# Thirty additions of a 31-tap convolution move from VectorE to GpSimd

## Chip, cores and metric

The kernel runs on one core of one Trainium2 chip. The metric is device time in microseconds of one execution; lower is better. All arithmetic is float32 or float32r, and all inputs start in HBM.

## What is computed

Two transformer blocks over the same 256 tokens of width 2048: the first with latent attention, sliding-window attention and an MLP, the second with a mixer, cross-attention and an MLP. The change lies in the mixer, whose one half is a depthwise convolution of width 31 over 1024 channels:

```python
def causal_depthwise_conv(x, w):
    """x (B, T, C), w (W, C): y[t, c] = sum_j w[j, c] * x[t - (W-1) + j, c] (zero left padding)."""
...
    c = glu[..., :D_CONV] * jax.nn.sigmoid(glu[..., D_CONV:])
    c = causal_depthwise_conv(c, cf_dw_w) + cf_dw_b
    c = jax.nn.silu(layer_norm(c, cf_ln_g, cf_ln_b))
    return jnp.concatenate([o, c], axis=-1) @ w_out
```

`o` is the other half: a gated delta rule over 8 heads, behind a convolution of width 4 on q, k and v.

## The kernel before, in words

**The stream of weights.** The time is spent on some 430 slots of weights, 1 MB each, loaded through SyncE's queue into `Wt`. A slot is worked off in two halves. For each half ScalarE makes a rounded copy `WH` (L1881), VectorE the remainder `WL` = `Wt` - `WH` (L2630), and TensorE multiplies three ways (L1267, L1268, L1269; L1305 and L1306 where the product is turned). `WH` and `WL` have four buffers (`NR = 4`), so the split of a half waits until TensorE has finished the half four before it.

**The order of the rest.** A planner (`Plan`) writes one list of steps; each engine's program walks the list and issues, in that order, what is its own of each step. Between two halves `pump` advances every background generator by one `yield`. All other work (norms, attention, convolutions, the delta rule) is such background, and it reaches an engine at a fixed place between the splits. An engine executes strictly in its program's order.

**The convolution.** `conv31` has steps k = 0 to 59. Step k is tap j = 1 + k // 2 on channel tiles 0 to 3 (g = 0, even k) or 4 to 7 (g = 1, odd k). The accumulator `AC` holds 8 tiles of 256 tokens. In `conv_tap` ScalarE writes w\*x of four tiles into a product buffer `PRD` (L2201), of which there are two; in `conv_add` VectorE adds it into `AC` (L3148), one planner step later. Above `SHARED` = 18 the odd steps don't use ScalarE: VectorE multiplies and adds each of the four tiles itself (L3153). So VectorE has 39 additions at L3148 (30 even steps, and the odd steps 1 to 17) and 84 at L3153. A generator variable `slow` sets how many halves lie between two steps: four at first, two near the end of `w_in_2`, one from the start of the delta rule. `cln_fold` sums `AC` when the last two steps are in.

**Neighbours in the same stretch.** While `w_in_2` streams, `qkv` runs six groups. In each, VectorE does three taps (L3167), ScalarE an exponential and a logarithm, VectorE a minimum (L3175, tile `QE`), ScalarE an exponential (L2251), VectorE a product (L3182), and for the q and k groups ScalarE a square (L2268) and TensorE a sum over channels (L1569); the two v groups go from L3182 straight to TensorE (L1559). While the next product streams, `gen_delta` inverts triangular blocks: TensorE (L1655), ScalarE (L2398) and VectorE (L3429, L3432) in turn, one short product after another between the halves. SyncE only issues loads and GpSimd's program is empty.

Of the kernel before, what the change touches and what calls it, by code (L numbers as in the profile page):

```python
# [16 lines left out]
ADD, SUB, MUL, MAX, MIN = ALU.add, ALU.subtract, ALU.mult, ALU.max, ALU.min  # L17
# [11 lines left out]
SHARED = 18  # L29
# [63 lines left out]
class Marks:  # L93
# [7 lines left out]
    def up(self, sig, *key, by=1, frees=None):  # L101
        n = self.count[sig] = self.count.get(sig, 0) + by
        self.value[(sig, *key)] = n
        for use in () if frees is None else frees if isinstance(frees, (list, tuple)) else (frees,):
            self.emptied.setdefault(use.n, {})[sig] = n
        return (self.sems and self.sems[sig]), by
# [12 lines left out]
    def at(self, sig, *key):  # L119
        if self.counted is None:  # L120
            return sig, None, 0
        return sig, self.sems[sig], self.counted.value[(sig, *key)]

    def last(self, sig):
        return sig, (self.sems and self.sems[sig]), self.count.get(sig, 0)
# [1086 lines left out]
    return [({"lnm1": "evwo.v", "lnxa": "evwo2.v", "lnm2": "evxo.v"}[nm], c, tb)]  # L1212

def q_tile(h):

    return sorted({(192 * h) // 512, (0, 0, 1, 1, 1, 2, 2, 2)[h]})
# [7 lines left out]
def tensor_program(pe, on, m, M, plan):  # L1225
# [243 lines left out]
    @named  # L1469
    def mla_turn(h, hq, b0, b1):  # L1470
        st, bk = f"mla{h % 6}", m.bank(b0)
        for s in freed(b0):
            on.wait_ge(*s)
        for c in q_tile(h):
            on.wait_ge(*at("evq.a", c))
            on.wait_ge(*at("evq.v", c))
        for tb in range(2):
            pe.transpose(bk[:, tb * P:(tb + 1) * P], m.Q[:, tb, 192 * h:192 * h + 128], ident)
        on.wait_ge(*at("rope.v", hq))
        for tb in range(2):  # L1480
            t = pe.transpose(bk[:, 256 + tb * P:256 + (tb + 1) * P], m.Q[:, tb, 192 * h + 64:192 * h + 192], ident)
        t.then_inc(*up(st + ".t", "queries", h))
        bk = m.bank(b1)
        on.wait_ge(*at("evkv.a", h // 2))
        on.wait_ge(*at("evkv.v", h // 2))
        for s in freed(b1):
            on.wait_ge(*s)
        for tb in range(2):
            t = pe.transpose(bk[:, tb * P:(tb + 1) * P], m.KV[:, tb, 256 * h:256 * h + 128], ident)
        t.then_inc(*up(st + ".t", "keys", h))  # L1490
# [344 lines left out]
def scalar_program(act, on, m, M, plan):  # L1835
    up, at, last, freed, dma = M.up, M.at, M.last, M.freed, M.dma
# [350 lines left out]
    @named  # L2187
    def conv_tap(k, j, g):
        if k > SHARED and g:
            return  # L2190
        if k == SHARED:
            on.wait_ge(*at("cconv.v", "added", k - 1))
        elif k > SHARED + 2:
            on.wait_ge(*at("cconv.v", "added", k - 4))
        elif k >= 2:
            on.wait_ge(*at("cconv.v", "added", k - 2))
        on.wait_ge(*at("mix.a", "turned", 1, 1))
        on.wait_ge(*at("prep.v", "columns"))
        for i in range(4):
            w = 8 * j + 4 * g + i  # L2200
            act.activation(m.products(k)[:, i, :], m.CP[:, 4 * g + i, j:j + 256], ACT.Copy, scale=m.CFW[:, w:w + 1]  # L2201
                           ).then_inc(*up("cconv.a", k))
# [380 lines left out]
def vector_program(dve, on, m, M, plan):  # L2583
    up, at, last = M.up, M.at, M.last
# [556 lines left out]
    @named  # L3141
    def conv_add(k, j, g):

        cs = slice(4 * g, 4 * g + 4)
        on.wait_ge(*(at("cconv.v", "added", k - 2) if k >= 2 else at("cconv.v", "first", g)))
        if k <= SHARED or g == 0:
            on.wait_ge(*at("cconv.a", k))
            dve.tensor_tensor(m.AC[:, cs, :], m.AC[:, cs, :], m.products(k)[:, :, :], ADD).then_inc(  # L3148
                *up("cconv.v", "added", k))
            return  # L3150
        for i in range(4, 8):
            w = 8 * j + i
            dve.scalar_tensor_tensor(m.AC[:, i, :], m.CP[:, i, j:j + 256], m.CFW[:, w:w + 1], m.AC[:, i, :], MUL, ADD  # L3153
                                     ).then_inc(*up("cconv.v", "added", k))
# [84 lines left out]
    @named  # L3239
    def cln_fold():  # L3240
        for k in (58, 59):
            on.wait_ge(*at("cconv.v", "added", k))
        dve.tensor_tensor(m.LNA[:, 0:4, :], m.AC[:, 0:4, :], m.AC[:, 4:8, :], ADD).then_inc(*up("cln.v"))
        on.wait_ge(*last("cln.v"))
        dve.tensor_tensor(m.LNA[:, 0:2, :], m.LNA[:, 0:2, :], m.LNA[:, 2:4, :], ADD).then_inc(*up("cln.v"))
        on.wait_ge(*last("cln.v"))
        dve.tensor_tensor(m.LNA[:, 0, :], m.LNA[:, 0, :], m.LNA[:, 1, :], ADD).then_inc(*up("cln.v", "folded"))
# [352 lines left out]
            step[name](*args)  # L3600

def sync_program(sp, on, m, M, plan):
    at, dma = M.at, M.dma
    A, step = m.A, {}
# [117 lines left out]
def build(nc, A, out):  # L3723
    m = Memory(nc, A, out)
    plan = plan_all(A)
    programs = (sync_program, scalar_program, vector_program, tensor_program)
    counted = Marks()
    for program in programs:
        program(Counting(), Waits(Counting()), m, counted, plan)
    with ExitStack() as ctx:  # L3730
        sems = {n: ctx.enter_context(nc.semaphore(n.replace(".", "_"))) for n in counted.count}
        M = Marks(counted, sems)
        block = ctx.enter_context(nc.Block())
        block.sync(lambda e: sync_program(e, Waits(e), m, M, plan))
        block.scalar(lambda e: scalar_program(e, Waits(e), m, M, plan))
        block.vector(lambda e: vector_program(e, Waits(e), m, M, plan))
        block.tensor(lambda e: tensor_program(e, Waits(e), m, M, plan))

NAMES = ["x", "positions", "rel_bias", "attn_norm", "w_in", "q_a_norm", "w_q_b", "kv_a_norm", "w_kv_b", "sinks",  # L3740
# [27 lines left out]
```

## Time and profile before

| what | value |
|---|---|
| median of 3 runs | 2580.25 us (2579.12 to 2581.32) |
| profiled execution | 2579.72 us |
| its span, first to last instruction | 2577.9 us |
| TensorE busy | 2550.9 us (99%) |
| VectorE busy | 1659.1 us (64%), 2130 instructions |
| ScalarE busy | 1332.1 us (52%) |
| GpSimd busy | 0.2 us, 4 instructions |
| granted TensorE clock | 0.998 |

Busy time counts an engine's instructions. Idle time before an instruction is put down to the instruction that released its semaphore; TensorE's records overlap a little, since its instructions are pipelined. The profile shows no time for the start of an execution and its end, 1.8 us here, beside the span. On VectorE, records overlap too: an addition of 128x1024 has 1.216 us on record, and the next instruction starts 1.14 us after it.

### The profile page before, as it was taken

Reading aid. Unit: us, or ns where it says so; the run is one execution under the profiler, and the core shown is the slowest. Engines: PE = TensorE matmul, PEld = TensorE weight load, DVE = VectorE, ACT = ScalarE, POOL = GpSimd, SP = SyncE. Lnnn points to the kernel's source line nnn. Section 1 sums busy time; section 2 is a strip of 40 time slices with the busy share of each in tenths; the row PEclk is TensorE's granted clock in tenths of the full one; section 3 lists DMA queues with packets and bytes.
Section 4 is the critical chain, followed back from the end, with each engine's and each line's share of the span. In section 5 each row is a group of like instructions: output and inputs, shape, how many; then the busy total and the mean of one; then the engine's idle time right before and its main releaser. Section 6 shows DMA issues by size and latency. Waiting matters only on the chain.

```text
span 2577.9 us, 33743 instructions
## 1 busy us (share of the span) xinstructions
PE 2550.9 (99%) x13752; PEld 2153.1 (84%) x13752; DVE 1659.1 (64%) x2130; ACT 1332.1 (52%) x1885; POOL 0.2 (0%) x4
## 2 busy tenths in 40 slices
PE   9999999999999999999999999999999999999998
PEld 8878888888888888887788888888888888888887
DVE  8686566655665567568887986544556555665565
ACT  6565554444444446568866665544554444444444
POOL 0000000000000000000000000000000000000000
PEclk9999999999999999999999999999999999999999
DMA  6534666565566555555453446544655556556554
GB/s 228 171 122 146 214 225 200 193 196 188 190 194 194 188 190 180 196 180 168 138 195 131 148 147 253 188 140 146 200 192 189 188 196 194 186 191 196 193 186 144
DMA packets 235041, 470.77 MB, mean 183 GB/s; under 512 B 8235, under 2 KB 17158, under 8 KB 233478
## 3 DMA queue, kind: packets, MB, share of 16 engines
q1 hardware_dynamic: 234134, 467.04, 55.0%
q8 instruction: 108, 1.77, 0.3%
q10 hardware_dynamic: 752, 1.58, 0.2%
q14 instruction: 47, 0.39, 0.0%
HBM read 462.30 MB, written 6.29 MB: 182 GB/s over the span
## 4 chain that ended last, share of the span: by engine, by line
PE 48%; DVE 1%; ACT 1%; issue 1%; DVEq 0%; ACTq 0%
PE ps L1267 10%; PE ps L1269 10%; PE ps L1268 10%; PE ps L1306 9%; PE ps L1305 5%; PE ps L1655 1%; PE ps L1826 1%; PE ps L1801 1%; PE ps L1338 0%; DVE WL L2630 0%; DVE AC L3153 0%; PE ps L1737 0%; ACT WH L1881 0%; PE ps L1638 0%; PE ps L1700 0%
## 5 line engine op out<-in xcount | busy, mean ns | idle before, releaser
L2630 DVE TENSOR_TENSOR WL<-Wt,WH 128x1024 fp32r<-128x1024 f32 (+1 forms) x861 | 1037.0, 1209 | 707.4 <-ACT WH L1881 651.7
L1881 ACT ACTIVATE WH<-Wt 128x1024 fp32r<-128x1024 f32 (+1 forms) x861 | 894.1, 1046 | 780.1 <-PE ps L1269 517.1
L1267 PE MATMUL ps<-WH,XT 128*128 128x512 f32 (+1 forms) x1184 | 470.6, 398 | 0.3 <-DVE XT L3028 0.3
L1267 PE MATMUL ps<-WH,HT 128*128 128x512 f32 (+2 forms) x1176 | 456.6, 388 | 3.3 <-DVE WL L2630 3.3
L1269 PE MATMUL ps<-WH,XT 128*128 128x512 f32 (+1 forms) x1184 | 459.8, 388 | 0.0
L1268 PE MATMUL ps<-WL,XT 128*128 128x512 f32 (+1 forms) x1184 | 459.3, 388 | 0.0
L1269 PE MATMUL ps<-WH,HT 128*128 128x512 f32 (+2 forms) x1176 | 451.4, 384 | 0.0
L1268 PE MATMUL ps<-WL,HT 128*128 128x512 f32 (+2 forms) x1176 | 451.0, 384 | 0.0
L1306 PE MATMUL ps<-XT,WH 128*128 128x512 f32 x960 | 336.5, 394 | 0.0
L1306 PE MATMUL ps<-HT,WH 128*128 128x512 f32 x960 | 336.5, 394 | 0.0
L1305 PE MATMUL ps<-XT,WL 128*128 128x256 f32 x960 | 266.6, 278 | 0.0
L1305 PE MATMUL ps<-HT,WL 128*128 128x256 f32 x960 | 266.6, 278 | 0.0
L1269 PEld LDWEIGHTS ps<-WH,XT 128*128 128x128 f32 x1184 | 222.6, 188 | 46.4
L1267 PEld LDWEIGHTS ps<-WH,XT 128*128 128x128 f32 x1184 | 222.8, 188 | 44.7 <-DVE XT L3028 0.7
L1267 PEld LDWEIGHTS ps<-WH,HT 128*128 128x128 f32 x1176 | 220.8, 188 | 46.4 <-DVE WL L2630 4.8
L1268 PEld LDWEIGHTS ps<-WL,XT 128*128 128x128 f32 x1184 | 223.0, 188 | 42.6
L1269 PEld LDWEIGHTS ps<-WH,HT 128*128 128x128 f32 x1176 | 220.7, 188 | 42.7
L1268 PEld LDWEIGHTS ps<-WL,HT 128*128 128x128 f32 x1176 | 220.9, 188 | 42.4 <-issue 1.0
L1306 PEld LDWEIGHTS ps<-XT,WH 128*128 128x128 f32 x960 | 180.0, 188 | 39.0
L1306 PEld LDWEIGHTS ps<-HT,WH 128*128 128x128 f32 x960 | 180.0, 188 | 39.0
L1305 PEld LDWEIGHTS ps<-HT,WL 128*128 128x128 f32 x960 | 180.3, 188 | 2.9
L1305 PEld LDWEIGHTS ps<-XT,WL 128*128 128x128 f32 x960 | 180.3, 188 | 2.9
(412 smaller groups left out, 1863.0 us busy)
## 6 DMA issues: line engine op xcount, KB each, us to landing
Wt<-in_mlp_w SPq DMA_DIRECT2D x128, 1024.0 KB, 5.1
Wt<-in_w_up SPq DMA_DIRECT2D x64, 1024.0 KB, 5.3
Wt<-in_w_down SPq DMA_DIRECT2D x64, 1024.0 KB, 5.0
Wt<-in_w_in SPq DMA_DIRECT2D x53, 1024.0 KB, 5.0
Wt<-in_w_out SPq DMA_DIRECT2D x32, 1024.0 KB, 5.0
Wt<-in_xa_wk SPq DMA_DIRECT2D x16, 1024.0 KB, 5.1
Wt<-in_xa_wv SPq DMA_DIRECT2D x16, 1024.0 KB, 5.0
Wt<-in_xa_wq SPq DMA_DIRECT2D x16, 1024.0 KB, 5.1
```

Source lines behind the costliest of these rows:

```text
L1267: pe.matmul(o, xh, wh, start=start, stop=False)
L1268: pe.matmul(o, xh, wl, start=False, stop=False)
L1269: done = pe.matmul(o, xl, wh, start=False, stop=stop)
L1305: pe.matmul(*(both if start else one), start=start, stop=False)
L1306: done = pe.matmul(*(one if start else both), start=False, stop=stop)
L1655: done = pe.matmul(m.bank(use)[r, 64 * h:64 * h + 64], left(r, h), right(r, h), start=True, stop=True)
L1801: t = pe.matmul(m.bank(b)[:, tb * 256:(tb + 1) * 256], m.QXT[:, u, k, tb * P:(tb + 1) * P], m.XKT[:, 4 * h + k, :], start=k == 0, stop=k == 3)
L1826: t = pe.matmul(m.bank(b)[:, i * 256:(i + 1) * 256], m.XV[:, mb, c:c + P], m.PXT[:, h % 2, mb, :], start=mb == 0, stop=mb == 1)
L1881: act.activation(m.WH[:, i % NR, 0:2 * w], m.Wt[:, slot % NW, h * 2 * w:(h + 1) * 2 * w], ACT.Copy).then_inc(*up("wsplit.a", i))
L2630: dve.tensor_tensor(m.WL[:, i % NR, 0:2 * w], m.Wt[:, slot % NW, h * 2 * w:(h + 1) * 2 * w], m.WH[:, i % NR, 0:2 * w].bitcast(F32), SUB).t ...
```

## The change

GpSimd gets a program of its own, `pool_program`. It walks the same list and does `conv_add` for the even steps (channel tiles 0 to 3), 30 additions of 128x1024, each counted on a new semaphore `cconv.p`. VectorE's `conv_add` returns at once for g = 0. ScalarE's `conv_tap` waits for the addition that last read its product buffer, on GpSimd's or VectorE's semaphore (`conv_added`), and `cln_fold` waits for step 58 on GpSimd's and 59 on VectorE's.

```diff
+def conv_added(k):
+    return "cconv.v" if k % 2 else "cconv.p", "added", k
...
         if k == SHARED:
-            on.wait_ge(*at("cconv.v", "added", k - 1))
-        elif k > SHARED + 2:
-            on.wait_ge(*at("cconv.v", "added", k - 4))
+            on.wait_ge(*at(*conv_added(k - 1)))
+        if k > SHARED + 2:
+            on.wait_ge(*at(*conv_added(k - 4)))
         elif k >= 2:
-            on.wait_ge(*at("cconv.v", "added", k - 2))
+            on.wait_ge(*at(*conv_added(k - 2)))
...
     def conv_add(k, j, g):
-        cs = slice(4 * g, 4 * g + 4)
+        if g == 0:
+            return
         on.wait_ge(*(at("cconv.v", "added", k - 2) if k >= 2 else at("cconv.v", "first", g)))
-        if k <= SHARED or g == 0:
+        if k <= SHARED:
             on.wait_ge(*at("cconv.a", k))
-            dve.tensor_tensor(m.AC[:, cs, :], m.AC[:, cs, :], m.products(k)[:, :, :], ADD).then_inc(
+            dve.tensor_tensor(m.AC[:, 4:8, :], m.AC[:, 4:8, :], m.products(k)[:, :, :], ADD).then_inc(
                 *up("cconv.v", "added", k))
...
     def cln_fold():
         for k in (58, 59):
-            on.wait_ge(*at("cconv.v", "added", k))
+            on.wait_ge(*at(*conv_added(k)))
...
+def pool_program(pool, on, m, M, plan):
+    up, at = M.up, M.at
+    def conv_add(k, j, g):
+        if g:
+            return
+        on.wait_ge(*(at("cconv.p", "added", k - 2) if k >= 2 else at("cconv.v", "first", 0)))
+        on.wait_ge(*at("cconv.a", k))
+        pool.tensor_tensor(m.AC[:, 0:4, :], m.AC[:, 0:4, :], m.products(k)[:, :, :], ADD).then_inc(
+            *up("cconv.p", "added", k))
+    for name, args in plan.steps:
+        if name == "conv_add":
+            conv_add(*args)
...
+        block.gpsimd(lambda e: pool_program(e, Waits(e), m, M, plan))
```

How the instructions stand. Lines of the changed kernel are 5 or 6 higher than the same ones before. First VectorE's program beside the second and third `qkv` group, where steps 3 and 4 of the convolution stood; `PRD0` holds even steps and `PRD1` odd ones here. Before:

```order
L2630 TENSOR_TENSOR WL_51<-Wt_49,WH_50 128x1024 [waits wsplit_a]
L3148 TENSOR_TENSOR AC_140<-AC_140,PRD1_149 128x1024 [waits cconv_a,cconv_v]
L3175 SCALAR_TENSOR_TENSOR QE1_146<-QA1_144,QE1_146 128x1024 [waits qkv_a]
...
L3182 TENSOR_TENSOR QA1_144<-QA1_144,QE1_146 128x1024 [waits qkv_a]
...
L2630 TENSOR_TENSOR WL_51<-Wt_49,WH_50 128x1024 [waits gemm_t,wsplit_a]
L3148 TENSOR_TENSOR AC_140<-AC_140,PRD0_148 128x1024 [waits cconv_a,cconv_v]
L3167 SCALAR_TENSOR_TENSOR QA0_143<-QC_142,DNW_58,QA0_143 128x256 [waits qkv_v] x4
```

and changed:

```order
L2635 TENSOR_TENSOR WL_51<-Wt_49,WH_50 128x1024 [waits wsplit_a]
L3154 TENSOR_TENSOR AC_140<-AC_140,PRD1_149 128x1024 [waits cconv_a,cconv_v]
L3181 SCALAR_TENSOR_TENSOR QE1_146<-QA1_144,QE1_146 128x1024 [waits qkv_a]
...
L3188 TENSOR_TENSOR QA1_144<-QA1_144,QE1_146 128x1024 [waits qkv_a]
...
L2635 TENSOR_TENSOR WL_51<-Wt_49,WH_50 128x1024 [waits gemm_t,wsplit_a]
L3173 SCALAR_TENSOR_TENSOR QA0_143<-QC_142,DNW_58,QA0_143 128x256 [waits qkv_v] x4
```

The even addition (from `PRD0`) is gone; the odd one still stands ahead of the minimum. Second, VectorE's program in the delta rule's second block, late in the convolution. Before:

```order
L2630 TENSOR_TENSOR WL_51<-Wt_49,WH_50 128x1024 [waits gemm_t,wsplit_a,wload1]
L3327 TENSOR_SCALAR KVS_165<-ps3,SM_65 128x512 [waits st_kx,gemm_t]
L3429 TENSOR_TENSOR XS5_159<-XS4_158,CST_55 128x512
L3432 TENSOR_TENSOR E0_162<-CST_55,ps6 128x512 [waits delta_t]
L3148 TENSOR_TENSOR AC_140<-AC_140,PRD1_149 128x1024 [waits cconv_a,cconv_v]
L2630 TENSOR_TENSOR WL_51<-Wt_49,WH_50 128x1024 [waits wsplit_a]
```

and changed:

```order
L2635 TENSOR_TENSOR WL_51<-Wt_49,WH_50 128x1024 [waits gemm_t,wsplit_a,wload1]
L3333 TENSOR_SCALAR KVS_165<-ps3,SM_65 128x512 [waits st_kx,gemm_t]
L3435 TENSOR_TENSOR XS5_159<-XS4_158,CST_55 128x512
L3438 TENSOR_TENSOR E0_162<-CST_55,ps6 128x512 [waits delta_t]
L2635 TENSOR_TENSOR WL_51<-Wt_49,WH_50 128x1024 [waits wsplit_a]
```

The addition behind `E0` is gone; what TensorE waits for (`E0`) stood ahead of it already. Third, GpSimd's new program from its start:

```order
L3618 ISA
L3618 TENSOR_TENSOR AC_140<-AC_140,PRD0_148 128x1024 [waits cconv_a,cconv_v]
L3618 TENSOR_TENSOR AC_140<-AC_140,PRD0_148 128x1024 [waits cconv_a,cconv_p] x8
L3618 TENSOR_TENSOR AC_140<-AC_140,PRD1_149 128x1024 [waits cconv_a,cconv_p]
L3618 TENSOR_TENSOR AC_140<-AC_140,PRD0_148 128x1024 [waits cconv_a,cconv_p]
```

An addition there is bound to no place among VectorE's instructions: it may start as soon as ScalarE's four products are written.

## Rows read from the trace of the kernel before

**Rows 1.** The page, busy time by engine: us, share of the span, instructions.
```profile
PE 2550.9 (99%) x13752; PEld 2153.1 (84%) x13752; DVE 1659.1 (64%) x2130; ACT 1332.1 (52%) x1885; POOL 0.2 (0%) x4
```

**Rows 2.** Tile PRD: duration ns min/median/max, first and last start us, forms.
```profile
L2201 ACT ACTIVATE PRD<-CP,CFW x156: 489/496/512, 1135.0 to 1484.6; 128x256 f32<-128x256 f32 x156
L3148 DVE TENSOR_TENSOR AC<-AC,PRD x39: 1212/1216/1225, 1147.9 to 1489.0; 128x1024 f32<-128x1024 f32 x39
```

**Rows 3.** Windows from 1147 us: busy us by engine, clock, DMA share, GB/s.
```profile
1147.00:1257.00 110.00, 110.00 (x495) 89.10 (x494) 90.14 (x118) 92.30 (x135) 0.00 (x0) 1.00 0.50 160
1340.00:1495.00 155.00, 153.06 (x1546) 126.78 (x1545) 135.56 (x195) 96.36 (x162) 0.00 (x0) 1.00 0.44 145
1147.00:1495.00 348.00, 340.52 (x2497) 287.13 (x2496) 292.35 (x407) 247.89 (x402) 0.00 (x0) 1.00 0.48 156
```

**Rows 4.** TensorE's waits, 1134 to 1552 us: total us, times, longest.
```profile
PE ps L1267 <- DVE WL L2630: 3.3, 4, 1.5
PE ps L1559 <- DVE QA L3182: 2.3, 2, 1.4
PE ps L1655 <- DVE XS L3421: 1.5, 1, 1.5
PE ps L1587 <- DVE LNA L3247: 1.3, 1, 1.3
PE ps L1761 <- DVE VT L3504: 1.0, 1, 1.0
PE ps L1737 <- DVE XS L3469: 0.5, 1, 0.5
```

**Rows 5.** Timeline, one qkv group, VectorE and ScalarE: start us, us, instruction [idle before].
```profile
1185.49 1.22 DVE L3148 TENSOR_TENSOR AC<-AC,PRD 128x1024 f32<-128x1024 f32 x1
1186.62 1.22 DVE L3175 SCALAR_TENSOR_TENSOR QE<-QA,QE 128x1024 f32<-128x1024 f32 x1
...
1184.22 1.70 ACT L2201 ACTIVATE PRD<-CP,CFW 128x256 f32<-128x256 f32 x4
...
1187.87 1.06 ACT L2251 ACTIVATE QE<-QE 128x1024 f32<-128x1024 f32 x1 [1.01 <-DVE QE L3175]
...
1193.29 1.06 ACT L2268 ACTIVATE QE<-QA 128x1024 f32<-128x1024 f32 x1
```

**Rows 6.** The same group on TensorE.
```profile
1194.87 1.88 PE L1569 MATMUL ps<-QE,CST 128*128 128x512 f32 x4
```

**Rows 7.** Timeline, delta rule, ScalarE and VectorE, 1465 to 1480 us.
```profile
1465.37 1.70 ACT L2201 ACTIVATE PRD<-CP,CFW 128x256 f32<-128x256 f32 x4
...
1474.38 1.70 ACT L2201 ACTIVATE PRD<-CP,CFW 128x256 f32<-128x256 f32 x4
...
1468.62 1.22 DVE L2630 TENSOR_TENSOR WL<-Wt,WH 128x1024 fp32r<-128x1024 f32 x1 [0.89 <-issue]
...
1471.02 0.68 DVE L3432 TENSOR_TENSOR E<-CST,ps 128x512 f32<-128x512 f32 x1
1471.62 1.22 DVE L3148 TENSOR_TENSOR AC<-AC,PRD 128x1024 f32<-128x1024 f32 x1
...
1477.11 1.23 DVE L2630 TENSOR_TENSOR WL<-Wt,WH 128x1024 fp32r<-128x1024 f32 x1 [0.95 <-issue]
...
1478.85 0.68 DVE L3432 TENSOR_TENSOR E<-CST,ps 128x512 f32<-128x512 f32 x1
```

**Rows 8.** The same stretch on TensorE: where it takes what L3432 made.
```profile
1471.75 1.15 PE L1655 MATMUL ps<-E,XS 64*64 64x64 f32 x32
...
1480.74 1.15 PE L1655 MATMUL ps<-E,XS 64*64 64x64 f32 x32
```

**Rows 9.** Timeline, VectorE, where narrow halves follow each other.
```profile
1268.68 1.22 DVE L3148 TENSOR_TENSOR AC<-AC,PRD 128x1024 f32<-128x1024 f32 x1
1269.82 1.66 DVE L3167 SCALAR_TENSOR_TENSOR QA<-QC,DNW,QA 128x256 f32<-128x256 f32 x4
1271.40 0.88 DVE L2630 TENSOR_TENSOR WL<-Wt,WH 128x704 fp32r<-128x704 f32 x1
```

More of the change, by code:

```diff
@@ L3725, in build @@
     plan = plan_all(A)
-    programs = (sync_program, scalar_program, vector_program, tensor_program)
+    programs = (sync_program, scalar_program, vector_program, tensor_program, pool_program)
     counted = Marks()
```

## Prediction

> **What bounds the kernel now.** I read the page first. TensorE is busy for 2550.9 of 2577.9 us and VectorE for 1659.1 [rows 1]: a microsecond taken off VectorE is worth something only where TensorE waits for it. So I read TensorE's waits in the stretch of the convolution: 3.3 + 2.3 + 1.5 + 1.3 + 1.0 + 0.5 = 9.9 us, all for VectorE [rows 4]. That is the most that a faster VectorE can give back. Then the windows: from the first addition to the last, VectorE is busy for 292.35 of 348 us, TensorE for 340.52 [rows 3]. VectorE is not the bound, but it has no more than 56 us to spare in 348, and TensorE's program takes many of its results in the middle of the stream. The question is then how much a handover can slip before TensorE feels it, and for that I read timelines.
>
> In a `qkv` group the reader should see a chain without slack. VectorE's minimum starts at 1186.62 and ends at 1187.84; ScalarE's exponential, which had stood idle for it for 1.01 us, starts at 1187.87; the product and the square follow, and the square ends at 1193.29 + 1.06 = 1194.35, 0.52 us ahead of TensorE's sum at 1194.87 [rows 5, 6]. A slip of the minimum by more than about half a microsecond therefore stands in TensorE's way. In the delta rule VectorE's L3432 ends at 1471.70 and TensorE takes it at 1471.75, a slack of 0.05 us; the next time it ends at 1479.53 and is taken at 1480.74, a slack of 1.21 us [rows 7, 8]. This pair repeats every 9 us or so.
>
> **The change, part by part.**
>
> *Taken from VectorE:* 30 of the 39 additions at L3148, 1.216 us each on record [rows 2], 1.14 us each from start to start (1268.68 to 1269.82 [rows 9]): 30 x 1.14 = 34 us less work. By itself this shortens the kernel only at the waits. One removed addition stands ahead of the narrow split at 1271.40 [rows 9], at the head of the 3.3 us of waits for `WL`: -1.1. The waits for L3421 (1.5) and for L3247, the fold of the convolution (1.3), each have removed additions right ahead on VectorE: -1.5 and -1.1. L3469: -0.5. Sum -4.2; the bounds are 0 and -9.9 [rows 4]. I take -5, since an earlier VectorE also starts ScalarE's answers earlier.
>
> *Put on GpSimd:* 30 additions of 128x1024 with both inputs in SBUF. The trace holds no work of this engine but four tiny fills [rows 1], so its price has to be bounded. Not under VectorE's 1.2 us for the same work [rows 2]. ScalarE passes the same elements with a single input in 1.70 us for four tiles [rows 5]. The additions read twice that, and I take twice VectorE's time, 2.4 us, as an estimate. Upwards, 3.6 us (three times VectorE's) is my bound. The engine itself is in no hurry: its additions come 24 us apart beside the `qkv` groups and 9.0 us apart in the delta rule (ScalarE's products at 1465.37 and 1474.38 [rows 7]), so at 2.4 us no product buffer is late, and what waits for it costs 0. Its start-up instruction runs at the beginning, over 1100 us ahead of the first addition: 0.
>
 The asymmetry speaks for it: what is freed is worth 5 us at best guess, and even a hold of half the addition, 1.2 us, eats all of the 1.14 us that the addition freed, and comes at a moment that ScalarE chooses and not VectorE's program.
>
> Where would the hold fall? Beside the `qkv` groups: ScalarE's product for an even step ends at 1184.22 + 1.70 = 1185.92 [rows 5]. GpSimd's addition then stands right ahead of the minimum at 1186.62, in every group, since both come every eight halves. The minimum is 2.4 us late, less the slack of 0.5: 1.9 us at TensorE. Six groups: 6 x 1.9 = 11.4 us. In the delta rule: 18 of the additions fall there, one for each 9 us. The first of the two shown would start at 1467.07, right ahead of the split due at 1468.62 [rows 7]; it ends at 1469.5, the split and L3432 behind it are 0.9 us late, and with a slack of 0.05 all of it reaches TensorE. Where VectorE is still busy when the products are done, the hold starts later and costs up to 1.4. The second would run from 1476.08 to 1478.5 against a split due at 1477.11: 1.4 us late, slack 1.21, so 0.2 at TensorE. The mean of 1.4 and 0.2 is 0.8: 18 x 0.8 = 14.4 us. The other six additions lie where halves follow each other with several microseconds in hand: 0. Sum of the holds 25.8 us; with the relief, 25.8 - 5 = +21 us.
>
> **The sum** against the profiled execution: 2579.7 + 21 = 2600.7 us. That execution is 0.5 us under the median of 2580.25, so 2601 us.
>
> The Trainium skill, SBUF — State Buffer, section Who interferes with whom, says that a VectorE instruction with two SBUF inputs contends with a GpSimd instruction that reads SBUF, whichever starts second being blocked for the whole of the first. No run here shows it so far; it is the upper end above. Its page GPSIMD Engine Reference, section 3.1, gives 4497 ns for such an addition of twice the length; half of that, 2.25 us as an estimate from that page, would make the holds 0.15 us shorter and the sum about 3 us less.
>
> **Rivals.**
>
> *1. No hold: VectorE is simply relieved.* For it: ScalarE's products beside busy VectorE stay within 489 to 512 ns [rows 2], so engines can work side by side on SBUF. Against it: nothing in the trace; that pair of engines just isn't shown. Mechanism: the 1.14 us gone ahead of the split at 1271.40, ahead of L3421 and ahead of the fold. Time: 2580.25 - 5 = 2575 us, at the very most 2570. It decides if a GpSimd addition delays VectorE by less than about 0.3 us. This is the case of the other sign.
>
> *2. The two share, and each is slowed.* A GpSimd addition beside VectorE costs it about 1.2 us, as much as it gave up. VectorE's sum is unchanged, but the delay comes ahead of the minimum and of L3432 where the freed addition had stood behind them. `qkv`: 1.2 - 0.5 = 0.7, six times 4 us; delta rule: 0.2 x 18 = 4; less 5: +3, 2583 us. This is no measurable difference: 0.2% of the time, 5.2 us, is about what a measurement of this kernel can tell from no change.
>
> *3. The hold is full and a GpSimd addition is longer.* At 3.6 us: 6 x 3.1 = 19, and in the delta rule 18 x 2.0 = 36, since slack covers none of what is added; less 5: +50, 2630 us. Beyond 8.9 us ScalarE would wait for product buffers too. Nothing in the trace speaks for it.
>
> **How the numbers follow.** Full hold at about 2.4 us, my forecast (2590 to 2613): 0.52. Rival 3: 0.12. Rival 2: 0.14, of which a third above 5.2 us. Rival 1: 0.22, of which two thirds gain over 5.2 us, since its -5 sits on that line and -9.9 is its end. Faster: 0.15. Slower: 0.52 + 0.12 + 0.04 = 0.68. Within 0.2%: 0.17. The range runs from 2573, which leaves out the last few in 100 of rival 1, to 2624, which leaves out most of rival 3.
>
> **What would show it.** In the profile after: 30 GpSimd additions of 2 to 2.6 us; VectorE's L3175 or the split next to it standing 1 to 2 us longer or later than its 1.22 us; new waits of TensorE at L1569 (none before) of about 2 us four times, and at L1655 of up to 1.4 us many times; VectorE's other rows unchanged. Wrong it is if VectorE's instructions beside a GpSimd addition start and end as before: then 2575. If TensorE's waits grow but the delay per addition is not near GpSimd's duration, the size was wrong, not the mechanism.

## The result and the profile after

| | before | changed |
|---|---|---|
| median of 4 runs each | 2580.3 us | 2602.73 us |
| span of the profiled execution | 2577.9 us | 2601.2 us |
| ratio, 95% interval | | 1.0091 [1.0079, 1.0103] |

The change makes the kernel slower by 0.9%, 22.4 us by the medians; 2601 us had been forecast. The page after, busy time by engine, against [rows 1]:

```profile
PE 2554.3 (98%) x13752; PEld 2153.5 (83%) x13752; DVE 1673.2 (64%) x2100; ACT 1331.8 (51%) x1885; POOL 80.9 (3%) x34
```

VectorE has 30 instructions less and 14 us more on record. The tile `PRD` shows both engines' additions (duration ns min/median/max), against [rows 2]:

```profile
L3618 POOL TENSOR_TENSOR AC<-AC,PRD x30: 2367/2404/4480, 1137.6 to 1507.8; 128x1024 f32<-128x1024 f32 x30
L3154 DVE TENSOR_TENSOR AC<-AC,PRD x9: 1217/1218/1219, 1161.9 to 1324.0; 128x1024 f32<-128x1024 f32 x9
```

A GpSimd addition takes twice VectorE's time. The second of the six qkv groups, VectorE's timeline with GpSimd's addition beside it, against [rows 5] (start us, us):

```profile
1188.15 1.22 DVE L3154 TENSOR_TENSOR AC<-AC,PRD 128x1024 f32<-128x1024 f32 x1
1189.29 3.43 DVE L3181 SCALAR_TENSOR_TENSOR QE<-QA,QE 128x1024 f32<-128x1024 f32 x1
1192.65 1.21 DVE L2635 TENSOR_TENSOR WL<-Wt,WH 128x1024 fp32r<-128x1024 f32 x1
```

```profile
1188.72 2.92 POOL L3618 TENSOR_TENSOR AC<-AC,PRD 128x1024 f32<-128x1024 f32 x1 [23.35 <-ACT PRD L2206]
```

GpSimd's instruction is dispatched at 1188.72, while VectorE adds; it has 2.92 us on record where one that meets nobody has 2.38, so it was kept waiting for about 0.5 us, until VectorE's addition was over at 1189.37. Then it is VectorE's turn: the minimum has 3.43 us on record in place of 1.22. It ends at 1192.72, 1.08 us after GpSimd's end at 1191.64: it did its own work only then. ScalarE and TensorE behind it, against [rows 5, 6]:

```profile
1192.76 1.06 ACT L2256 ACTIVATE QE<-QE 128x1024 f32<-128x1024 f32 x1 [3.23 <-DVE QE L3181]
```

```profile
1199.27 1.99 PE L1574 MATMUL ps<-QE,CST 128*128 128x512 f32 x4 [1.57 <-ACT QE L2273]
```

That is the whole mechanism in one piece: hold, late minimum, late exponential, late square, TensorE idle. The minimum is struck in all six groups (ns):

```profile
L3181 DVE SCALAR_TENSOR_TENSOR QE<-QA,QE x6: 3386/3422/3434, 1163.0 to 1290.3; 128x1024 f32<-128x1024 f32 x6
```

Before, it read

```profile
L3175 DVE SCALAR_TENSOR_TENSOR QE<-QA,QE x6: 1215/1217/1218, 1162.2 to 1281.0; 128x1024 f32<-128x1024 f32 x6
```

TensorE's waits over the whole execution, total, times, longest, against [rows 4] (the largest, and the last ones of the stretch):

```profile
PE ps L1272 <- DVE WL L2635: 8.1, 5, 3.7
PE ps L1660 <- DVE E L3438: 7.0, 6, 2.0
PE ps L1574 <- ACT QE L2273: 6.3, 4, 1.6
PE ps L1660 <- DVE XS L3420: 2.4, 2, 2.1
PE ps L1564 <- DVE QA L3188: 1.9, 1, 1.9
...
PE ps L1766 <- DVE VT L3510: 1.0, 1, 1.0
PE ps L1592 <- DVE LNA L3253: 1.0, 1, 1.0
PE ps L1660 <- DVE XS L3427: 0.7, 2, 0.4
...
PE ps L1742 <- DVE XS L3475: 0.5, 1, 0.5
```

The nine sum to 28.9 us where [rows 4] had 9.9: 19.0 of the span's 23.3. Of the rest, 0.8 us lies before the convolution, in the start of this execution. Most of the remainder stands at the waits themselves: at the first sum TensorE idles for 1.59 us on record and falls 2.0 us behind. One stretch at the lower clock level adds a little, of which more below.

Where the time came from is best seen by when TensorE begins the same half of weights in both traces. The table holds that shift in us against the kernel before, worked out from one execution of each: the start of TensorE's first weight load of the half after, less the same before; ahead of the convolution (first column) it shows what an execution's start differs by. Times in the heading are those of the kernel before.

| kernel | 1124 us | 1172 | 1262 | 1288 | 1342 | 1445 | 1506 | end |
|---|---|---|---|---|---|---|---|---|
| changed | 0.8 | 2.7 | 10.0 | 11.9 | 11.9 | 20.2 | 23.0 | 23.2 |
| e2_none | -1.0 | -1.0 | -1.0 | -2.2 | -2.2 | -2.1 | -4.0 | -3.8 |
| e1_writes | -1.1 | -1.1 | -1.1 | -0.8 | -0.8 | -0.8 | -2.7 | -2.5 |
| e6_early | 0.7 | 2.6 | 9.9 | 12.0 | 12.0 | 12.0 | 12.0 | 12.0 |
| e7_late | -0.4 | -0.4 | -0.4 | -0.4 | -0.4 | 9.3 | 12.1 | 12.1 |
| e4_after_product | -1.1 | -1.1 | 1.2 | 4.6 | 6.1 | 14.4 | 17.3 | 17.3 |
| e8_gate | -1.5 | -1.4 | 1.0 | 2.5 | 2.5 | 7.0 | 8.1 | 8.1 |
| e5_quarters | 0.3 | 0.5 | 1.7 | 3.0 | 3.0 | 6.4 | 9.9 | 9.9 |
| e9_one_input | 0.5 | 1.1 | 2.8 | 4.0 | 4.0 | 4.0 | 2.1 | 2.3 |
| e10_gate_quarters | 1.1 | 1.1 | 2.9 | 4.2 | 4.2 | 5.8 | 8.0 | 8.0 |
| e11_twice | 0.3 | 2.3 | 12.3 | 14.4 | 21.0 | 52.0 | 68.4 | 68.6 |

The changed kernel loses 9.2 us in five steps of 1.6 to 2.0 us, one for each qkv group up to 1262 us, 1.9 more with the sixth, nothing up to 1342, and 11.1 us in the delta rule. There the loss is uneven: TensorE's waits range from 0.3 to 2.2 us, and several of the 18 additions cause none.

### The profile page after: what moved, and what is told of

It reads as the page before. It is cut to its first block and busy times, and to the rows that moved or that the text cites. A ratio compares the mean times of both kernels' runs of the same rounds, so it can differ in the third digit from the quotient of the medians.

```text
span 2601.2 us, 33746 instructions
## 1 busy us (share of the span) xinstructions
PE 2554.3 (98%) x13752; PEld 2153.5 (83%) x13752; DVE 1673.2 (64%) x2100; ACT 1331.8 (51%) x1885; POOL 80.9 (3%) x34
## 5 line engine op out<-in xcount | busy, mean ns | idle before, releaser
L2635 DVE TENSOR_TENSOR WL<-Wt,WH 128x1024 fp32r<-128x1024 f32 (+1 forms) x861 | 1056.2, 1232 | 715.0 <-ACT WH L1886 655.1
```

The lines of the kernel that those rows point to most:

```text
L2635: dve.tensor_tensor(m.WL[:, i % NR, 0:2 * w], m.Wt[:, slot % NW, h * 2 * w:(h + 1) * 2 * w], m.WH[:, i % NR, 0:2 * w].bitcast(F32), SUB).t ...
```

## The experiments

All are edits of the changed kernel; the name in brackets is the one in the table. Each was timed beside the kernel before, and its ratio is to that: medians of 2579.07 us for `e2_none`, `e1_writes`, `e6_early` and `e4_after_product`, 2578.73 us for `e9_one_input`, `e7_late`, `e8_gate` and `e5_quarters`, 2579.85 us for the last two. Against the changed kernel's 2602.73 us, taken beside 2580.3 us, they are best compared by what each is above its own.

**Take the additions away, leave the signals** (`e2_none`). The edit:

```diff
-        pool.tensor_tensor(m.AC[:, 0:4, :], m.AC[:, 0:4, :], m.products(k)[:, :, :], ADD).then_inc(
-            *up("cconv.p", "added", k))
+        pool.nop().then_inc(*up("cconv.p", "added", k))
```

> GpSimd's program keeps its waits and its signals, but the 30 additions of channel tiles 0 to 3 are left out on every engine, so the convolution of those tiles lacks taps 1 to 30. What is left is the relief of VectorE alone. Hold theory (a GpSimd addition keeps VectorE's instructions with two SBUF inputs waiting): about 2575 us, 5 under before, and all of the 27 us up to the changed kernel's 2602.7 is what the additions on GpSimd cost. Rival (the new semaphores and the other order of waits cost the time, not the additions): it stays near 2600.

Measured: 2577.14 us, ratio to before 0.999 [0.9981, 0.9999]. The new semaphores and orders cost nothing; all of the loss is what the additions do on GpSimd. The relief by itself is small, 2.8 us by the table and 1.9 us by the medians. TensorE's waits in the stretch, total, times, longest:

```profile
PE ps L1272 <- DVE WL L2635: 2.6, 2, 1.5
PE ps L1564 <- DVE QA L3188: 2.3, 2, 1.4
PE ps L1766 <- DVE VT L3510: 1.0, 1, 1.0
PE ps L1592 <- DVE LNA L3253: 1.0, 1, 1.0
PE ps L1742 <- DVE XS L3475: 0.5, 1, 0.5
```

Against [rows 4], only the wait for L3421 (1.5) went as a whole; the splits gave 0.7 on record (1.1 by the shift) and the fold 0.3.

**Keep GpSimd busy, but let it only write** (`e1_writes`).

```diff
-        pool.tensor_tensor(m.AC[:, 0:4, :], m.AC[:, 0:4, :], m.products(k)[:, :, :], ADD).then_inc(
+        for _ in range(2):
+            pool.memset(m.AC[:, 0:4, :], 0.0).then_inc(*up("cconv.p"))
+            on.wait_ge(*M.last("cconv.p"))
+        pool.memset(m.AC[:, 0:4, :], 0.0).then_inc(
             *up("cconv.p", "added", k))
```

> Each GpSimd addition is replaced by three fills of the same 128x1024 in a row, each waited for: GpSimd is as busy in the same places, writes SBUF but reads nothing from it. The sums of tiles 0 to 3 are left out. If what holds VectorE is the reading of SBUF by GpSimd: no VectorE row is stretched and the time is that of the kernel without additions, about 2575 us. If any GpSimd access to SBUF holds it (rival): VectorE's minimum takes 1.2 us plus the rest of a fill, and with fills of 1 us each the time is 2585 to 2600.

Measured: 2578.22 us, ratio 0.9996 [0.9987, 1.0005], 1.1 us above the kernel without additions. GpSimd was as busy as with additions (86 us of fills), and the minimum was not touched, though it ran beside the fills:

```profile
1184.94 1.97 POOL L3620 MEMSET AC<- 128x1024 f32 x2 [21.44 <-ACT PRD L2207]
1186.97 0.96 POOL L3622 MEMSET AC<- 128x1024 f32 x1
```

```profile
1185.54 1.22 DVE L3182 SCALAR_TENSOR_TENSOR QE<-QA,QE 128x1024 f32<-128x1024 f32 x1
```

So it is GpSimd's reading of SBUF that holds the minimum, not its work and not its writing. No other instruction of VectorE with 128x256 elements or more was longer beside a fill either. But writing alone is not free: three small instructions for the delta rule's gates are stretched beside the fills of the sixth group. A `TENSOR_SCALAR` of 128x16 with a single input in SBUF lasts until the fill ends, twice:

```profile
1279.92 0.59 DVE L3205 TENSOR_SCALAR SM<-SM 128x16 f32<-128x16 f32 x1
...
1280.57 0.95 DVE L3210 TENSOR_SCALAR SM<-SM 128x16 f32<-128x16 f32 x1
```

```profile
1278.52 1.97 POOL L3620 MEMSET AC<- 128x1024 f32 x2 [17.57 <-ACT PRD L2207]
1280.55 0.95 POOL L3622 MEMSET AC<- 128x1024 f32 x1
```

Without additions the first of them reads

```profile
1279.97 0.17 DVE L3204 TENSOR_SCALAR SM<-SM 128x16 f32<-128x16 f32 x1
```

The split behind them is 1.1 us late, and TensorE waits 2.6 us for it where it waited 1.5. That is most of the 1.4 us by which the table parts the two kernels at 1288 us, and as much as parts their medians, which the intervals don't separate. A stretch at the lower clock level follows in this execution, of which below.

**Read one input in place of two** (`e9_one_input`).

```diff
-        pool.tensor_tensor(m.AC[:, 0:4, :], m.AC[:, 0:4, :], m.products(k)[:, :, :], ADD).then_inc(
+        pool.tensor_scalar(m.AC[:, 0:4, :], m.products(k)[:, :, :], 1.0, None, MUL).then_inc(
             *up("cconv.p", "added", k))
```

> Each GpSimd addition is replaced by a multiplication by 1.0 of the product buffer into the same tiles of AC: one SBUF input in place of two, the sum of tiles 0 to 3 is left out. If GpSimd's reading holds VectorE for as long as the instruction runs, the cost follows its duration: at 1.3 us a hold of about 1.1, qkv groups 6 x 0.7, delta rule about 3, relief 5: 2580 to 2586 us. If only an instruction with two inputs holds VectorE (rival): 2575 us and no VectorE row is stretched.

Measured: 2580.48 us, ratio 1.0005 [0.9996, 1.0015]. That lies in the 2580 to 2586 us expected, and can't be told from the kernel before. The reason given does not hold, though. The instruction is longer than the addition, and holds less:

```profile
L3618 POOL TENSOR_SCALAR AC<-PRD x30: 2770/2777/4841, 1137.4 to 1487.7; 128x1024 f32<-128x1024 f32 x30
```

```profile
L3181 DVE SCALAR_TENSOR_TENSOR QE<-QA,QE x6: 2058/2060/2062, 1162.7 to 1283.1; 128x1024 f32<-128x1024 f32 x6
```

```profile
1187.10 3.28 POOL L3618 TENSOR_SCALAR AC<-PRD 128x1024 f32<-128x1024 f32 x1 [21.63 <-ACT PRD L2206]
```

The minimum is held for 0.84 us, and its work is done at 1189.72, 0.66 us before GpSimd's instruction ends at 1190.38. For this instruction the hold ends well before its end; with two inputs it lasted until the end. Why is not shown.

**Only early, only late** (`e6_early`, `e7_late`). A function decides by k which engine adds an even step; VectorE has the others as before.

```diff
+def on_pool(k):
+    return k % 2 == 0 and k <= 12        # e7_late: k >= 14
...
-        on.wait_ge(*(at("cconv.v", "added", k - 2) if k >= 2 else at("cconv.v", "first", g)))
+        on.wait_ge(*(at(*conv_added(k - 2)) if k >= 2 else at("cconv.v", "first", g)))
```

> GpSimd takes the even steps up to 12 only; VectorE has those from 14 on as before. The convolution's additions beside the qkv groups are then the only ones on GpSimd. Sum of the prediction: 6 holds of 1.9 us less about 1 us of relief, +10 us, 2590 us (the trace of the changed kernel has +9 to +11 there). Rival (cost spread evenly over the 30 additions): 7/30 of 22.4, +5 us, 2585.

> GpSimd takes the even steps from 14 on only, 23 additions; those beside the qkv groups are on VectorE as before. Place theory: the delta rule's share of the changed kernel, +11 to +12 us, 2592 us, and with the early half (GpSimd for steps up to 12) it adds up to the +22 of both. Rival (even spread): 23/30 of 22.4, +17 us, 2597.

Measured: 2591.08 us (ratio 1.0045 [1.0030, 1.0060]) and 2591.14 us (1.0044 [1.0028, 1.0061]). Seven additions beside the qkv groups cost as much as 23 later ones: place counts, not number. The shifts of 11.3 and 12.5 us from the convolution's start add up to 23.8, the changed kernel's is 22.4. TensorE's largest waits, early first:

```profile
PE ps L1578 <- ACT QE L2277: 6.3, 4, 1.6
```

```profile
PE ps L1664 <- DVE E L3443: 7.1, 6, 2.0
```

**Move the hold behind the product** (`e4_after_product`).

```diff
         on.wait_ge(*at("cconv.a", k))
+        if 2 <= k <= 12:
+            on.wait_ge(*at("qkv.v", "mul", k // 2 - 1))
```

> Beside the six qkv groups (steps 2 to 12) GpSimd's addition also waits for VectorE's product of that group, so it can no longer stand ahead of the minimum. The hold falls on the split and the taps of the next group, where there are some 3 us in hand. Place theory: the five steps of 1.8 us at TensorE's sums vanish, about 9 us less than the changed kernel, 2593 to 2595 us, no wait at the sum over channels. Rival (what counts is VectorE's total of work and hold, wherever the hold falls): within 3 us of 2602.7.

Measured: 2597.21 us, ratio 1.0073 [1.0056, 1.0090]: 5.5 us less than the changed kernel, and 18.1 above its own before in place of 22.4, so 4 rather than 9 us less. The minimum is back at its old length, and the waits at the sums go from 6.3 to 1.4 us:

```profile
L3181 DVE SCALAR_TENSOR_TENSOR QE<-QA,QE x6: 1217/1220/1220, 1161.1 to 1283.6; 128x1024 f32<-128x1024 f32 x6
```

```profile
PE ps L1584 <- DVE SM L3224: 1.7, 1, 1.7
PE ps L1574 <- ACT QE L2273: 1.4, 3, 0.6
```

By the table the shift up to 1262 us is 2.3 in place of 9.2. But from there to 1342 it is 4.9 in place of 1.9: where narrow halves follow each other VectorE has nothing in hand, and a hold hurts anywhere. A new wait of 1.7 us, for a small result of the gates, is part of it, and the last 1.5 us are a stretch at the lower clock level right behind that wait.

**Start no earlier than VectorE did** (`e8_gate`). VectorE notes its newest signal where it added before, and GpSimd waits for it.

```diff
         if g == 0:
+            M.gate[k] = M.newest
             return
...
         on.wait_ge(*at("cconv.a", k))
+        if M.counted:
+            sig, n = M.counted.gate[k]
+            on.wait_ge(sig, M.sems[sig], n)
```

> Each GpSimd addition also waits for the VectorE instruction ahead of which... behind which VectorE did that addition before. It can no longer start early in the middle of a chain; VectorE loses up to 2.4 us where it had spent 1.14. Place theory: the qkv share vanishes (the taps follow, with slack) and of the delta rule's share the part stays in which VectorE is behind anyway: +3 to +8 us, 2583 to 2588. Rival (total of hold counts): 2600.

Measured: 2587.98 us, ratio 1.0035 [1.0022, 1.0048], at the end of what was expected. Same additions, same hold (four taps take 3.82 us in place of 1.67), but 9.3 us above its own before in place of 22.4:

```profile
1197.00 3.82 DVE L3176 SCALAR_TENSOR_TENSOR QA<-QC,DNW,QA 128x256 f32<-128x256 f32 x4
```

**Cut each addition in four** (`e5_quarters`).

```diff
-        pool.tensor_tensor(m.AC[:, 0:4, :], m.AC[:, 0:4, :], m.products(k)[:, :, :], ADD).then_inc(
-            *up("cconv.p", "added", k))
+        for i in range(4):
+            t = pool.tensor_tensor(m.AC[:, i, :], m.AC[:, i, :], m.products(k)[:, i, :], ADD)
+        t.then_inc(*up("cconv.p", "added", k))
```

> Each GpSimd addition is cut into four of 128x256. If a hold lasts for one GpSimd instruction and VectorE gets in between two of them, a VectorE instruction is held by 0.7 us at most at a time: a minimum of 1.2 us takes at most 2 us on record, the slack of 0.5 covers most, and the time is 2585 to 2592. If GpSimd keeps VectorE out over its whole queue of four (rival), the row of the minimum shows 3.4 us or more and the time is 2602 to 2606, a bit above the changed kernel for the four starts.

Measured: 2588.55 us, ratio 1.0036 [1.0023, 1.0049], 9.8 us above its own before. The engines take turns: four quarters need 5.31 us, and each of VectorE's two instructions beside them is held by 0.54 us:

```profile
1186.56 5.31 POOL L3619 TENSOR_TENSOR AC<-AC,PRD 128x256 f32<-128x256 f32 x4 [19.32 <-ACT PRD L2206]
```

```profile
1187.12 1.76 DVE L3181 SCALAR_TENSOR_TENSOR QE<-QA,QE 128x1024 f32<-128x1024 f32 x1
1188.81 1.76 DVE L2635 TENSOR_TENSOR WL<-Wt,WH 128x1024 fp32r<-128x1024 f32 x1
```

A hold of 0.54 is about the slack of 0.5 us that the chain had, and up to 1262 us the shift is 1.4 us in place of 9.2.

**Both mendings** (`e10_gate_quarters`, the two edits above together).

> Both mendings at once: each addition in four of 128x256, and none before VectorE has reached the place where it did that addition before. If a late start and a short hold save different parts, less than either alone (2588.0 and 2588.6 us): 2581 to 2585. If they save the same part (rival), 2587 or 2588. Under the kernel before by more than 0.2% by neither: the kernel without any additions on GpSimd was only 2 us under it.

Measured: 2585.76 us, ratio 1.0024 [1.0014, 1.0033]: 5.9 us above its own before, 2 to 4 us better than either edit alone, 1 us above the expected stretch, and still slower than before. No version with these additions on GpSimd came under the kernel before.

**Each addition twice** (`e11_twice`).

```diff
+        pool.tensor_tensor(m.AC[:, 0:4, :], m.AC[:, 0:4, :], m.products(k)[:, :, :], ADD).then_inc(*up("cconv.p"))
+        on.wait_ge(*M.last("cconv.p"))
         pool.tensor_tensor(m.AC[:, 0:4, :], m.AC[:, 0:4, :], m.products(k)[:, :, :], ADD).then_inc(
```

> Each GpSimd addition is done twice, the second once the first has signalled, so tiles 0 to 3 get each product twice. Hold theory: VectorE gets in between the two (as it does between quarters), so the minimum shows 3.4 us as before and the instruction behind it is held as well, 2.4 us. In the qkv groups that hits a split with 3 us in hand, in the delta rule mostly a split that L3432 stands behind. The cost grows by more than a quarter and less than double: 2610 to 2630 us. Rival (what costs is that the first addition cuts in at a bad moment, later ones are free): under 2607.

Measured: 2650.06 us, ratio 1.0273 [1.0257, 1.0288]: three times the cost, where less than double was expected. Beside the qkv groups the second addition cost little: the shift up to 1262 us is 12.0 in place of 9.2. The miss is in the delta rule, 47.4 us in place of 11.1, with 6.6 more between 1288 and 1342 us, where single additions had cost nothing. TensorE's largest waits:

```profile
PE ps L1272 <- DVE WL L2635: 21.2, 9, 5.7
PE ps L1660 <- DVE E L3438: 21.2, 10, 2.8
```

VectorE now falls behind with the splits as well, and the windows (busy us of PE, PEld, DVE, ACT, POOL, then the granted clock) show a second cost:

```profile
1147.00:1540.00 393.00, 341.85 (x2294) 285.19 (x2294) 340.41 (x361) 239.46 (x388) 158.32 (x55) 0.95 0.41 136
```

The clock is granted at 0.95 where [rows 3] have 1.00. Over 393 us that is worth up to 20 us. In the delta rule the record has seven stretches at 1.2 GHz, 27.3 us long in all, and while they last the shift grows by some 11.6 us. So about a quarter of the 47.4 us is clock and the rest is waits.

## Why the prediction was right

*The bound.* TensorE's waits for VectorE, 9.9 us, were to be the most that relief can give. It gave 2.8 us (shift of e2_none), forecast at 5. Of the four terms, the split's 1.1 came (by the shift) and L3421 gave its 1.5; the fold gave 0.3 in place of 1.1, L3469 nothing, and the 0.8 added on top for ScalarE's earlier answers wasn't there. Ahead of the fold the waiting moved on to another input: in `e2_none` VectorE stands idle for 0.73 us until TensorE has the results that its copy L3447 takes. Ahead of L3469 no addition stood at all; VectorE had been idle for 4.6 us before the split and the one instruction that stand ahead of it.

*GpSimd's price.* 2.4 us was taken, 2.38 to 2.40 measured. Its first addition had 4.48 us, and a split dispatched 1.0 us after that one's start was not held (1.22 us); why is open. The additions come as close as 3.5 us in the delta rule, not every 9.0 us, and ScalarE still never waits for one. Rival 3 (3.6 us) is out.

*The hold.* Full, as taken: 3.42 us for the minimum. It begins when VectorE's own addition is over, so 2.2 of the 2.4 us fall on the minimum. The choice of the upper end is now a measured one; when it was made it rested on asymmetry alone. Rival 1 (no hold) and rival 2 (shared, 1.2 us each) are out by that row, and only without additions did the time come near rival 1's 2575 us.

The Trainium skill, SBUF — State Buffer, section Who interferes with whom, states the contention for VectorE instructions with two SBUF inputs against GpSimd instructions that read SBUF, not against those that only write: the trace agrees on both halves (3.42 us beside additions, 1.22 beside fills). The section calls the shared ports an exclusive lock, and writes of blocking for the whole instruction where it treats VectorE's 2-port modes. That whoever starts second is blocked for the whole of the first agrees for the addition, but not for the one-input instruction, whose 2.78 us held VectorE for 0.84.

*Beside the qkv groups.* 6 x 1.9 = 11.4 us was the term. Measured 9.2 for five groups and 1.9 net with the sixth, 11.1 in all. The slack of 0.5 us read from one group's timeline held for the four q and k groups, where TensorE waits 1.57 to 1.59 us at the sum. The fifth and sixth have no sum: there the split behind the minimum came late (waits of 1.45 us, and of 3.66 where it had been 1.50), and that the cost is about the same is luck. Luck is in the 2.4 us too: an addition from 1185.92 on would end at 1188.32, 1.7 us after the minimum was due, not 2.4. The rest came because VectorE's odd addition kept GpSimd's waiting first, which the prediction does not say.

*In the delta rule.* 18 x 0.8 = 14.4 us less most of the relief was the term, 11.1 measured net. At the first of the two sample places the hold fell on the four instructions of VectorE's odd step at L3159, 3.78 us in place of 1.66, not on the split behind them, and TensorE waited 1.08 us for `E` (1.4 forecast). At the second the split was held (2.57 us), and `E` still came in time (0.2 forecast):

```profile
1487.33 3.78 DVE L3159 SCALAR_TENSOR_TENSOR AC<-CP,CFW,AC 128x256 f32<-128x256 f32 x4
...
1499.52 2.57 DVE L2635 TENSOR_TENSOR WL<-Wt,WH 128x1024 fp32r<-128x1024 f32 x1 [2.09 <-issue]
...
1502.62 0.67 DVE L3438 TENSOR_TENSOR E<-CST,ps 128x512 f32<-128x512 f32 x1
```

```profile
1494.16 1.15 PE L1660 MATMUL ps<-E,XS 64*64 64x64 f32 x32 [1.08 <-DVE E L3438]
...
1503.35 1.15 PE L1660 MATMUL ps<-E,XS 64*64 64x64 f32 x32
```

The mean of two places came out right for the whole, though single waits reach 2.15 us and several additions cost nothing.

*The other six* were to cost nothing, and did: one addition lies ahead of the first qkv group, five between 1288 and 1342 us, where the shift stays at 11.9 although they hold VectorE too.

The sum: holds 25.8 forecast, 25.2 measured (22.4 + 2.8 of shift); relief 5 forecast, 2.8 measured. A hold 0.6 us too large makes up for part of a relief 2.2 us too large, and the forecast is 1.6 us short.

## What to carry to other kernels

Work moved from VectorE to GpSimd is not free work on an idle engine: while a GpSimd addition reads SBUF, VectorE's next instruction with two SBUF inputs stands still, so 1.14 us freed was paid with 2.2 us at a moment that the program's order doesn't choose. Before such a move, find where GpSimd's instruction will start (its releaser, not its place in the plan) and what VectorE instruction stands there, and read the slack from it to TensorE. If it must be done, short GpSimd instructions started behind the tight handover cost a quarter of long early ones (5.9 against 22.4 us). Fills left VectorE's large instructions alone; what they held were small ones of the gates, 1.1 us at TensorE.

## What the runs showed of the hardware beyond what was expected

*Only some VectorE instructions are held.* Beside GpSimd additions, those with one input in PSUM kept their length: the four at L3394 (`XS` from `ps` and `XS`), two of them started within an addition, and `E` from `CST` and `ps` at 1405.5 us:

```profile
L3394 DVE TENSOR_TENSOR XS<-ps,XS x4: 674/679/684, 1337.6 to 1448.4; 128x512 f32<-128x512 f32 x4
```

A single input doesn't protect where it is in SBUF: the small `TENSOR_SCALAR` of the gates was held by fills (0.95 us in place of 0.17), and by the additions of `e11_twice` for 2.14 us.

*The hold of a one-input GpSimd instruction is shorter than the instruction* (0.84 us at the minimum, of 2.78).

*TensorE's idle time can come back as a lower clock.* After its longest wait, 3.66 us, the changed kernel shows a stretch at 1.2 in place of 2.4 GHz, 3.4 us long by the clock's record and 0.79 of full speed in the window of 8 us around it; matmuls of 352 columns go from 0.32 to 0.50 us. The kernel before has none there.

```profile
1295.12 0.43 PE L1272 MATMUL ps<-WH,HT 128*128 128x352 f32 x1 [3.66 <-DVE WL L2635]
1295.39 0.38 PE L1273 MATMUL ps<-WL,HT 128*128 128x352 f32 x1
1295.56 0.50 PE L1274 MATMUL ps<-WH,HT 128*128 128x352 f32 x1
```

```profile
1292.00:1300.00 8.00, 4.88 (x25) 4.82 (x25) 6.82 (x14) 5.96 (x14) 0.57 (x1) 0.79 0.34 104
```

At half speed for 3.4 us it could cost 1.7 us. Here the shift grows by 1.1 us in it, and a wait for `QA` of 0.90 us, which the kernel before has right behind, takes nearly all of that up. In `e7_late`, where no such wait follows, a stretch cost 1.5 us. One execution each is no proof that the wait brings it about. The fills' execution had such a stretch too, at 1282 us in a wait of 2.6 us, and the one without additions, whose longest wait was 1.5 us, had none in the convolution. But the length of the wait does not decide alone: stretches follow waits of 1.68 us (`e4_after_product`) and 1.93 us (`e7_late`), and waits of 1.95 and 2.15 us in the changed kernel have none behind them. In `e11_twice`, with waits up to 5.7 us, it became a cost of its own.
